# Rotating queries and keys with VectorE's lane shuffle and a GpSimd product instead of TensorE's permutation product

## The chip, the cores and the metric

One core of a Trainium2 chip runs the whole kernel. The time is in device microseconds for one execution. Everything is float32. A large matrix product is made of three products of parts that TensorE takes in one pass each (a high part of weight and input, and a low part of each).

## The reference, cut to what matters

One inference step of a layer with two branches, block-sparse attention with 8 heads of 128 channels and an mLSTM with 4 heads of 256. There are 256 prompt tokens and 8 sample tokens, 264 in all, and the samples attend to a paged cache of 1024 tokens. The change touches one step only, the rotation of normalised queries and keys:

```python
def partial_rope(x, pos):
    half = ROT_DIM // 2                      # ROT_DIM = 32 of 128 channels
    ...
    x1, x2 = xf[..., :half], xf[..., half:ROT_DIM]
    out = jnp.concatenate([x1 * cos - x2 * sin, x2 * cos + x1 * sin, xf[..., ROT_DIM:]], axis=-1)

aq = partial_rope(rms_norm(aq.reshape(B, S, ATT_HEADS, ATT_HD), q_norm_w), pos)
ak = partial_rope(rms_norm(ak.reshape(B, S, ATT_HEADS, ATT_HD), k_norm_w), pos)
```

Only the first 32 of a head's 128 channels are rotated. Channel m of the first 16 is paired with channel m + 16.

## The kernel before, in words

Activations lie with the channels on the 128 partitions and the 264 tokens (`T`) along the free dimension, so a rotation pairs partitions. Each engine has its own list of instructions, and semaphores order them.

**Projections.** 112 blocks of weights (512 KB each, 128 output channels) come in by SyncE's DMA queue, eight ahead. ScalarE splits off the high part (`split_hi`, line 829), VectorE the low part (`split_lo`, line 1082), both three blocks or so ahead of TensorE's 24 products (`project`, lines 545 and 548). ScalarE copies each result out of PSUM and counts `evac`.

**Head stage** (to about 50 us). Blocks 0 to 7 are the eight query heads. For head h ScalarE writes the scaled query to `qT[:, h, :]` and its square to `sq`. One block later, `norm_sums` on TensorE multiplies the square with a matrix of ones (line 553, the sum over the channels) and the query with the permutation `rot` (line 554), and counts `norm_ps`. ScalarE makes the inverse norm `rs` (lines 849 and 850, `rs_ready`). VectorE's `rope_norm` then multiplies the permuted query by the sine (line 1120) and the query by the cosine (1121), adds (1122) and multiplies by the inverse norm (1123), and counts `q_ready`. Between the heads VectorE also works on the gate rows (heads 1 to 3), and at head 3 it counts `rows_ready`. TensorE's product for head g waits for `q_ready` of head g - 2, since it writes the same bank.

After the heads, TensorE projects block 8 and then, in `beside(0)`, waits for `q_ready` of all eight heads and transposes the queries of the sample tokens (line 498).

**GpSimd's list.** After `proj` reaches 2 it issues four key pages and seven value pages of the cache (`keys`, `values`, by line 418), then waits for `rows_ready`, stores the gate rows to DRAM (line 458), waits for that store (`row_put`), loads one row of each kind back to partition 0 (`decay_rows`, lines 442 and 443), waits for these loads and spreads them over the partitions (`spread_rows`, 447 and 448). Then it waits for the sample queries (`qs_ready`), stores them and spreads the first one (465), issues the last value page and enters a loop over the projections, in which it issues the pages for the samples that follow, their queries and the gate rows of the next rounds.

**Four rounds** of 16 projections (lines numbered by i = 0 to 15) follow, each with two attention heads and one mLSTM head: the keys are blocks i = 0 and 1, `keys_side` on TensorE forms their sums and permutation at i = 1 and 3, and VectorE rotates them in `rope_norm` at i = 2 and 4 into `kT[:, n, :]` (`kT_ready`). The tile `hT` holds the sine product in `hT[:, 0, :]`; later in each round it holds mLSTM outputs, until `mlg_ready` is counted. VectorE also scores the cache pages against the sample queries (line 1181) and updates the samples' states (1263). The last 40 projections follow.

Of the kernel before, what the change touches and what calls it, by code (L numbers as in the profile page):

```python
# [33 lines left out]
HEADS = 8  # L34
# [11 lines left out]
ROT = HD // 4  # L46
THETA = 500000.0
# [97 lines left out]
def build(nc, a, o):  # L145
    ctx = ExitStack()
    with ctx:
# [142 lines left out]
        blank, blank_eye = sem("blank"), sem("blank_eye")  # L290
        xsq_act, xsq_dve, xn_ready = sem("xsq_act"), sem("xsq_dve"), sem("xn_ready")
# [108 lines left out]
        def _(pool):  # L400
# [50 lines left out]
            pool.wait_ge(proj, 2)  # L451
            for s in range(KSLOTS):
                keys(s)
            for s in range(VSLOTS - 1):
                values(s)

            pool.wait_ge(rows_ready, 1)
            pool.dma_start(rows_dram, rows[:, :, :].rearrange("p a t -> p (a t)")).then_inc(row_put, 16)
            pool.wait_ge(row_put, 16)
            decay_rows(0)  # L460
# [11 lines left out]
            for g in range(LAST):  # L472
                b = due(g, SELECT)
                if b is not None:
                    pool.wait_ge(mx_ready, b + 1)
                    nc.gpsimd.partition_all_reduce(gmax[:, b, :], mx[:, b % 2, :], P, bass.bass_isa.ReduceOp.max).then_inc(gmax_ready, 1)
                s = key_page(g)
                if s is not None:
                    if s + KSLOTS < NB * PAGES:
                        keys(s + KSLOTS)  # L480
                    if s % PAGES == 0 and 2 <= s // PAGES + 1 < NB:
                        queries(s // PAGES + 1)
                    if s % PAGES == 2 and s // PAGES + 1 < NB:
                        spread_queries(s // PAGES + 1)
                for s in value_loads(g):
                    values(s)
                if g % CHUNKS == 13 and g // CHUNKS + 1 < JOBS:
                    decay_rows(g // CHUNKS + 1)
                if g % CHUNKS == 14 and g // CHUNKS + 1 < JOBS:
                    spread_rows(g // CHUNKS + 1)  # L490
# [3 lines left out]
        def _(pe):  # L494
# [56 lines left out]
            def norm_sums(ss, ro, i, src):  # L551

                mm(ss[:, 0:T], ones, sq[:, i, :], start=True, stop=True)
                mm(ro[:, 0:T], rot, src, start=True, stop=True).then_inc(norm_ps, 1)


            for h in range(HEADS + 1):
# [4 lines left out]
                if h >= 1:  # L562
                    g = h - 1
                    pe.wait_ge(evac, g + 1)
                    if g == 0:
                        pe.wait_ge(boot_r, 16)
                    if g >= 2:
                        pe.wait_ge(q_ready, g - 1)
                    norm_sums(wk[2 * (g % 2)], wk[2 * (g % 2) + 1], g % 2, qT[:, g, :])
# [8 lines left out]
            def keys_side(j, i):  # L578

                if i in (1, 3):  # L580
# [8 lines left out]
                    norm_sums(wk[2 * n], wk[2 * n + 1], n, kT[:, n, :])  # L589
# [486 lines left out]
        def _(dve):  # L1076
# [41 lines left out]
            def rope_norm(x, r, ro, done):  # L1118

                ch.step(V.tensor_tensor(hT[:, 0, :], ro[:, 0:T], sin, ALU.mult))  # L1120
                ch.link(V.tensor_tensor(x, x, cos, ALU.mult))
                ch.link(V.tensor_tensor(x, x, hT[:, 0, :], ALU.add))
                V.tensor_tensor(x, x, r, ALU.mult).then_inc(done, 1)

            for h in range(HEADS):
# [16 lines left out]
                dve.wait_ge(norm_ps, h + 1)  # L1142
                dve.wait_ge(rs_ready, h + 1)
                rope_norm(qT[:, h, :], rs[:, h % 2, :], wk[2 * (h % 2) + 1], q_ready)
# [76 lines left out]
            def keys_side(j, i):  # L1221

                if i in (2, 4):
                    n = i // 2 - 1
                    dve.wait_ge(norm_ps, HEADS + 2 * j + n + 1)
                    dve.wait_ge(rs_ready, HEADS + 2 * j + n + 1)

                    dve.wait_ge(mlg_ready, j)
                    rope_norm(kT[:, n, :], rs[:, n, :], wk[2 * n + 1], kT_ready)
# [222 lines left out]
def constants():  # L1452
# [5 lines left out]
    for m in range(half):  # L1458
        c[m + half, C_ROT + m] = -1.0
# [10 lines left out]
    for s in range(2):  # L1470
        c[s * half:(s + 1) * half, C_COS:C_COS + T] = np.cos(ang)
        c[s * half:(s + 1) * half, C_SIN:C_SIN + T] = np.sin(ang)
# [70 lines left out]
```

## Time and profile before

| | us |
|---|---|
| median of three runs (lowest to highest) | 468.84 (468.48 to 469.5) |
| the profiled execution | 469.01 |
| its span, first to last instruction | 466.9 |
| TensorE busy | 455.6 (98%) |
| VectorE busy | 393.8 (84%) |
| ScalarE busy | 290.5 (62%) |
| GpSimd busy | 100.5 (22%) |
| DMA engines, mean over the span | 323 GB/s |

The granted clock of TensorE is full throughout. In the names of the profile PE is TensorE, PEld its weight loads, DVE is VectorE, ACT is ScalarE, POOL is GpSimd and SP is SyncE; SPq, ACTq and POOLq are their queues of DMA issues and register work. Instructions that an engine merely issues to its DMA queue are not counted as busy. A float32 product takes TensorE two records (x2 in the counts).

### The profile page before, as it was taken

To read this page: it belongs to the slowest core of one execution; us is meant where nothing else is said; L and a number is where in the kernel's file an instruction comes from. 1 tells how busy PE (TensorE), PEld (TensorE's weight loads), DVE (VectorE), ACT (ScalarE), POOL (GpSimd) and SP (SyncE) were. 2 spreads that over 40 slices of the span, in tenths; PEclk is the share of its full clock that TensorE was granted. 3 is DMA by queue.
4 is the path that set the end of the run, shared out by engine and by line. 5 is a ranking of instruction groups with operands and counts; after the bars stand their busy time and mean duration, and the time that the engine had idled before them with its cause. 6 is when DMAs were issued, how large, how long until landed. Compare 5 with 4: busy or idle time off the path is not lost.

```text
span 466.9 us, 11342 instructions
## 1 busy us (share of the span) xinstructions
PE 455.6 (98%) x3855; PEld 414.0 (89%) x3855; DVE 393.8 (84%) x1610; ACT 290.5 (62%) x487; POOL 100.5 (22%) x181
## 2 busy tenths in 40 slices
PE   6999999999999999999999999999999999999997
PEld 4899899897879789888899889889898899899997
DVE  4898899699999799999899999889999946568861
ACT  4866545676984496896485695667958346324430
POOL 2040421013323213422321242312222201000000
PEclk9999999999999999999999999999999999999999
DMA  8899699749999999999999999998999995447511
GB/s 306 324 355 406 173 349 363 237 156 336 320 416 408 388 360 352 412 412 408 409 384 297 405 413 409 411 384 285 403 415 410 409 382 182 162 149 261 181 49 48
DMA packets 44858, 150.91 MB, mean 323 GB/s; under 512 B 6192, under 2 KB 7796, under 8 KB 44672
## 3 DMA queue, kind: packets, MB, share of 16 engines
q1 hardware_dynamic: 20368, 70.77, 41.0%
q0 software_dynamic: 19008, 67.20, 37.4%
q10 hardware_dynamic: 5424, 12.21, 6.9%
q8 instruction: 31, 0.51, 0.4%
q14 instruction: 27, 0.22, 0.1%
HBM read 137.37 MB, written 12.76 MB: 322 GB/s over the span
## 4 chain that ended last, share of the span: by engine, by line
PE 66%; ACT 12%; DVE 9%; DMA 7%; issue 4%; ACTq 1%; SPq 0%; DVEq 0%; POOLq 0%
PE pj L545 25%; PE pj L548 12%; PE wk L545 8%; PE pa L728 4%; PE wk L548 4%; DMA kpages<-in_cache_k 4%; ACT whi L829 3%; DVE kpages L1181 2%; DMA out_C_s<-cslot 2%; ACT L849 2%; DVE wlo L1082 2%; DVE cslot L1263 1%; PE wk L498 1%; PE wk L650 1%; PE wk L684 1%
## 5 line engine op out<-in xcount | busy, mean ns | idle before, releaser
L545 PE MATMUL pj<-xn,whi 128*128 128x264 f32 x1328 | 180.8, 289 | 1.6 <-ACT mqT L987 1.3
L545 PEld LDWEIGHTS pj<-xn,whi 128*128 128x128 f32 x1328 | 168.5, 189 | 10.2 <-issue 6.2
L1082 DVE TENSOR_TENSOR wlo<-wraw,whi 128x1024 fp32r<-128x1024 f32 x112 | 136.2, 1219 | 9.5 <-ACT whi L829 9.1
L829 ACT ACTIVATE whi<-wraw 128x1024 fp32r<-128x1024 f32 x112 | 117.9, 1053 | 21.0 <-PE wk L548 13.5
L1181 DVE CUSTOM_DVE_ANT_0 kpages<-kpages,qbc 128x128 f32<-128x128 f32 x512 | 116.3, 292 | 3.5 <-DMA kpages<-in_cache_k 3.3
L548 PE MATMUL pj<-xn,wlo 128*128 128x264 f32 x664 | 93.9, 284 | 0.7 <-DVE wlo L1082 0.7
L548 PEld LDWEIGHTS pj<-xn,wlo 128*128 128x128 f32 x664 | 85.4, 188 | 1.1 <-DVE wlo L1082 1.1
L418 POOL DMA_DIRECT2D kpages<-in_cache_k x64 | 34.3, 536 | 167.4 <-DVE sco L1181 145.1
L418 POOL DMA_DIRECT2D vpages<-in_cache_v x64 | 33.9, 530 | 60.6 <-issue 38.4
L1181 DVE DVE_READ_ACCUMULATOR2_ANT sco<- 128x1 f32 x512 | 42.1, 82 | 0.0
L728 PE MATMUL pa<-vpages,prob 128*32 128x256 f32 x512 | 33.8, 384 | 1.9 <-ACT prob L887 1.9
L1263 DVE SCALAR_TENSOR_TENSOR cslot<-wk,kc,cslot 128x256 f32<-128x256 f32 x64 | 26.5, 476 | 1.7 <-PE wk L700 1.7
L545 PE MATMUL wk<-xn,whi 128*128 128x264 f32 x192 | 25.9, 287 | 0.0
L728 PEld LDWEIGHTS pa<-vpages,prob 128*32 128x32 f32 x512 | 13.6, 109 | 13.8 <-issue 3.1
L545 PEld LDWEIGHTS wk<-xn,whi 128*128 128x128 f32 x192 | 24.3, 189 | 1.2 <-issue 1.2
L877 ACT ACTIVATE cslot<-cslot,bcg 128x512 f32<-128x512 f32 x32 | 21.2, 711 | 0.0
L922 ACT ACTIVATE att<-att,rsum 128x128 f32<-128x128 f32 x8 | 3.2, 403 | 26.4 <-DVE rsum L1244 26.4
L545 PE MATMUL wk<-mlg,whi 128*128 128x264 f32 x128 | 17.0, 285 | 0.0
L545 PEld LDWEIGHTS wk<-mlg,whi 128*128 128x128 f32 x128 | 16.0, 188 | 0.5 <-issue 0.4
L545 PE MATMUL pj<-mlg,whi 128*128 128x264 f32 x112 | 14.8, 284 | 0.0
L545 PEld LDWEIGHTS pj<-mlg,whi 128*128 128x128 f32 x112 | 14.1, 188 | 0.4 <-issue 0.4
L548 PE MATMUL wk<-xn,wlo 128*128 128x264 f32 x96 | 13.5, 283 | 0.0
(270 smaller groups left out, 609.5 us busy)
## 6 DMA issues: line engine op xcount, KB each, us to landing
wraw<-in_weights SPq DMA_DIRECT2D x112, 512.0 KB, 6.7
kpages<-in_cache_k POOLq DMA_DIRECT2D x64, 512.0 KB, 8.4
vpages<-in_cache_v POOLq DMA_DIRECT2D x64, 512.0 KB, 11.1
cslot<-in_states SPq DMA_DIRECT2D x16, 512.0 KB, 8.8
out_C_s<-cslot ACTq DMA_DIRECT2D x16, 512.0 KB, 8.1
xres<-in_tokens SPq DMA_DIRECT2D x1, 1056.0 KB, 5.6
out_k_p<-kT ACTq DMA_DIRECT2D x4, 256.0 KB, 10.0
out_v_p<-v_nat ACTq DMA_DIRECT2D x4, 256.0 KB, 5.1
```

Source lines behind the costliest of these rows:

```text
L418: return pool.dma_start(tile, src)
L498: return nc.tensor.transpose(out, in_, ident[0:rows_, 0:rows_])
L545: mm(bank[:, 0:T], whi[:, q, k, :], src[:, g, k, :], start=(k == 0 and g == 0), stop=False)
L548: last = mm(bank[:, 0:T], wlo[:, n % WRAW, k, :], src[:, 0, k, :], start=False, stop=(k == KC - 1))
L650: mm(wk[1][g * VC:(g + 1) * VC, 0:MHD], qmask[:, d, b * VC:(b + 1) * VC], cslot[:, b, d, :], start=(half == 0 and d == 0), stop=(half == 1 ...
L728: last = mm(pv[q * VC:(q + 1) * VC, 0:VW], prob[:, b % 2, first:first + VC], vpages[:, s % VSLOTS, q * VW:(q + 1) * VW], start=(pg == 0), ...
L829: A(whi[:, n % WSPLIT], wraw[:, n % WRAW], ACT.Copy).then_inc(whi_ready, 1)
L849: ch.link(A(dst, ss, ACT.Ln, scale=1.0 / width, bias=epsc))
L877: A(cslot[:, b], cslot[:, b], ACT.Copy, scale=bcg[:, 0, j, b:b + 1]).then_inc(fade_ready, 1)
L1082: V.tensor_tensor(wlo[:, n % WRAW], wraw[:, n % WRAW], whi[:, n % WSPLIT], ALU.subtract).then_inc(wlo_ready, 1)
L1181: last = V.tensor_tensor_reduce(k, k, qbc[:, b % 2, h * HD:(h + 1) * HD], 1.0, 0.0, ALU.mult, ALU.add, sco[:, b % 2, pg, h:h + 1])
L1263: last = V.scalar_tensor_tensor(out=cslot[:, b, d, :], in0=row, scalar=kc[:, d, b:b + 1], in1=cslot[:, b, d, :], op0=ALU.mult, op1=ALU.add)
```

## The change

The product with `rot` goes. Instead VectorE shuffles the first 32 partitions with `stream_shuffle`, whose table `SWAP` exchanges the two halves, into `hT[0:32, 0, :]`, and multiplies this by the sine, which carries the sign now. GpSimd multiplies the first 32 partitions by the cosine into `hT[0:32, 1, :]` and counts the new semaphore `scaled`. VectorE waits for `scaled`, adds, waits for `rs_ready`, and multiplies all 128 partitions by the inverse norm. Shuffle and sine product wait for `evac` only.

Since there is one tile for the cosine product, GpSimd waits for the head before to be done (`q_ready`, `kT_ready`) first. GpSimd's other work of the head stage, which stood in one block, is dealt out between the eight products: two pages after each of heads 1 to 5 and one after head 6, the store of the gate rows after head 5's pages, the wait for that store and the two row loads after head 6's page, then head 7's product. TensorE's sum for head g now waits for `rs_ready`.

```diff
+SWAP = [(m + ROT // 2) % ROT for m in range(ROT)]
...
-            pool.wait_ge(proj, 2)
-            for s in range(KSLOTS):
-                keys(s)
-            for s in range(VSLOTS - 1):
-                values(s)
-
-            pool.wait_ge(rows_ready, 1)
-            pool.dma_start(rows_dram, rows[:, :, :].rearrange("p a t -> p (a t)")).then_inc(row_put, 16)
-            pool.wait_ge(row_put, 16)
-            decay_rows(0)
+            pool.wait_ge(blank, 6)
+            pool.wait_ge(boot_r, 16)
+            for h in range(HEADS):
+
+                pool.wait_ge(evac, h + 1)
+                if h:
+                    pool.wait_ge(q_ready, h)
+                pool.tensor_tensor(hT[0:ROT, 1, :], qT[0:ROT, h, :], cos[0:ROT], ALU.mult).then_inc(scaled, 1)
+                if h in (1, 2):
+                    for s in range(KSLOTS // 2):
+                        keys(KSLOTS // 2 * (h - 1) + s)
+                if h in (3, 4, 5, 6):
+                    for s in range(2 * (h - 3), min(2 * (h - 2), VSLOTS - 1)):
+                        values(s)
+                if h == 5:
+                    pool.wait_ge(rows_ready, 1)
+                    pool.dma_start(rows_dram, rows[:, :, :].rearrange("p a t -> p (a t)")).then_inc(row_put, 16)
+                if h == 6:
+                    pool.wait_ge(row_put, 16)
+                    decay_rows(0)
             spread_rows(0)
...
             for g in range(LAST):
+                if g < BODY and g % CHUNKS in (1, 3):
+                    j, n = g // CHUNKS, g % CHUNKS // 2
+                    pool.wait_ge(mlg_ready, j)
+                    pool.wait_ge(kT_ready, 2 * j + n)
+                    pool.wait_ge(evac, HEADS + j * CHUNKS + n + 1)
+                    pool.tensor_tensor(hT[0:ROT, 1, :], kT[0:ROT, n, :], cos[0:ROT], ALU.mult).then_inc(scaled, 1)
...
-                    if g == 0:
-                        pe.wait_ge(boot_r, 16)
                     if g >= 2:
-                        pe.wait_ge(q_ready, g - 1)
-                    norm_sums(wk[2 * (g % 2)], wk[2 * (g % 2) + 1], g % 2, qT[:, g, :])
+                        pe.wait_ge(rs_ready, g - 1)
+                    mm(wk[2 * (g % 2)][:, 0:T], ones, sq[:, g % 2, :], start=True, stop=True).then_inc(norm_ps, 1)
...
-                    norm_sums(wk[2 * n], wk[2 * n + 1], n, kT[:, n, :])
+                    mm(wk[2 * n][:, 0:T], ones, sq[:, n, :], start=True, stop=True).then_inc(norm_ps, 1)
...
-            def rope_norm(x, r, ro, done):
-
-                ch.step(V.tensor_tensor(hT[:, 0, :], ro[:, 0:T], sin, ALU.mult))
-                ch.link(V.tensor_tensor(x, x, cos, ALU.mult))
-                ch.link(V.tensor_tensor(x, x, hT[:, 0, :], ALU.add))
+            def rope(x, r, n, done):
+
+                ch.link(V.stream_shuffle(hT[0:ROT, 0, :], x[0:ROT], SWAP))
+                ch.step(V.tensor_tensor(hT[0:ROT, 0, :], hT[0:ROT, 0, :], sin[0:ROT], ALU.mult))
+                ch.join()
+                dve.wait_ge(scaled, n + 1)
+                ch.link(V.tensor_tensor(x[0:ROT], hT[0:ROT, 0, :], hT[0:ROT, 1, :], ALU.add))
+                dve.wait_ge(rs_ready, n + 1)
                 V.tensor_tensor(x, x, r, ALU.mult).then_inc(done, 1)
...
                 dve.wait_ge(boot_r, 16)
-                dve.wait_ge(norm_ps, h + 1)
-                dve.wait_ge(rs_ready, h + 1)
-                rope_norm(qT[:, h, :], rs[:, h % 2, :], wk[2 * (h % 2) + 1], q_ready)
+                dve.wait_ge(evac, h + 1)
+                rope(qT[:, h, :], rs[:, h % 2, :], h, q_ready)
...
-                    dve.wait_ge(norm_ps, HEADS + 2 * j + n + 1)
-                    dve.wait_ge(rs_ready, HEADS + 2 * j + n + 1)
-
+                    dve.wait_ge(evac, HEADS + j * CHUNKS + n + 1)
                     dve.wait_ge(mlg_ready, j)
-                    rope_norm(kT[:, n, :], rs[:, n, :], wk[2 * n + 1], kT_ready)
+                    rope(kT[:, n, :], rs[:, n, :], HEADS + 2 * j + n, kT_ready)
...
-        c[s * half:(s + 1) * half, C_SIN:C_SIN + T] = np.sin(ang)
+        c[s * half:(s + 1) * half, C_SIN:C_SIN + T] = (2 * s - 1) * np.sin(ang)
```

## Rows read from the trace of the kernel before

**Rows 1.** the page, part 1: busy us of each engine (share), x instructions
```profile
PE 455.6 (98%) x3855; PEld 414.0 (89%) x3855; DVE 393.8 (84%) x1610; ACT 290.5 (62%) x487; POOL 100.5 (22%) x181
```

**Rows 2.** the page, part 4: the chain that ended last, by engine
```profile
PE 66%; ACT 12%; DVE 9%; DMA 7%; issue 4%; ACTq 1%; SPq 0%; DVEq 0%; POOLq 0%
```

**Rows 3.** TensorE's groups by shape: tiles, shapes, count, busy us, mean ns
```profile
L554 PE MATMUL wk<-qT,cst 128*128 128x264 f32 x16 | 4.9, 386 | 0.0
L554 PE MATMUL wk<-kT,cst 128*128 128x264 f32 x16 | 4.9, 386 | 0.0
```

**Rows 4.** the chain by time, 40 to 62 us: start us, us, what
```profile
43.32 0.46 PE wk L554 x2
...
47.89 0.44 DVE qT L1123
...
53.25 0.45 PE wk L554 x2
```

**Rows 5.** timeline, 20 to 50 us: start us, us, engine, line, what
```profile
21.60 0.57 POOL L418 DMA_DIRECT2D kpages<-in_cache_k  x1 [14.34 <-issue]
...
33.51 0.53 POOL L418 DMA_DIRECT2D vpages<-in_cache_v  x1 [0.62 <-issue]
...
34.77 0.52 POOL L458 DMA_DIRECT2D rows_dram<-rows  x1 [0.73 <-DVEq L1140]
...
48.38 0.60 PE L498 MATMUL pa<-cst,qT 128*8 128x128 f32 x4 [0.52 <-DVE qT L1123]
...
49.32 0.51 POOL L442 DMA_DIRECT2D decay<-rows_dram  x1 [14.03 <-DMA rows_dram<-rows]
```

**Rows 6.** DMA issues, 20 to 60 us, median landing; then landings, kpages, vpages
```profile
rows_dram<-rows POOLq DMA_DIRECT2D x1, 8.0 KB, 14.3
...
DMA to landing us min/median/max: 4.4/7.2/8.7
...
DMA to landing us min/median/max: 5.1/11.7/15.2
```

**Rows 7.** timeline of ScalarE and VectorE in the head stage
```profile
21.65 0.42 ACT L850 ACTIVATE rs<-rs 128x264 f32<-128x264 f32 x1
21.98 1.05 ACT L829 ACTIVATE whi<-wraw 128x1024 fp32r<-128x1024 f32 x1
...
23.95 1.23 DVE L1082 TENSOR_TENSOR wlo<-wraw,whi 128x1024 fp32r<-128x1024 f32 x1
...
38.81 0.43 DVE L1123 TENSOR_TENSOR qT<-qT,rs 128x264 f32<-128x264 f32 x1
```

**Rows 8.** timeline at 53 us; then ns min/median/max of two operations
```profile
53.36 1.22 DVE L1082 TENSOR_TENSOR wlo<-wraw,whi 128x1024 fp32r<-128x1024 f32 x1
53.38 2.36 POOL L465 PARTITION_BROADCAST qbc<-qs  x1
...
54.50 1.21 DVE L1166 TENSOR_TENSOR gexp<-wN,cst 8x96 f32<-8x96 f32 x1
...
L434 POOL PARTITION_BROADCAST qbc<-qbc x7: 1294/1300/1468, 69.0 to 315.7; - x7
...
L1193 DVE TENSOR_TENSOR pairs<-gpad x8: 257/258/260, 99.9 to 383.6; 128x96 f32<-128x96 f32 x8
```

**Rows 9.** groups of GpSimd, first microseconds: busy us, mean ns
```profile
L403 POOL MEMSET qmask<- 128x512 f32 x1 | 0.5, 524 | 0.0
L404 POOL MEMSET mvs<- 128x256 f32 x1 | 0.3, 311 | 0.0
```

**Rows 10.** windows: length, busy us (x count), clock, DMA share, GB/s
```profile
28.00:32.00 4.00, 4.00 (x32) 3.84 (x30) 3.83 (x8) 2.81 (x7) 1.59 (x3) 1.00 1.01 408
...
120.00:130.00 10.00, 9.74 (x87) 7.54 (x85) 9.95 (x44) 9.88 (x15) 4.01 (x7) 1.00 0.93 321
```

**Rows 11.** the chain by time, round 1: start us, us, what
```profile
126.66 1.28 ACT L849
...
137.52 0.45 DVE kT L1123
```

More of the change, by code:

```diff
@@ L290, in build @@
         blank, blank_eye = sem("blank"), sem("blank_eye")
+        scaled = sem("scaled")
         xsq_act, xsq_dve, xn_ready = sem("xsq_act"), sem("xsq_dve"), sem("xn_ready")
@@ L549, in project @@
                 last.then_inc(proj, 1)
-            def norm_sums(ss, ro, i, src):
-                mm(ss[:, 0:T], ones, sq[:, i, :], start=True, stop=True)
-                mm(ro[:, 0:T], rot, src, start=True, stop=True).then_inc(norm_ps, 1)
             for h in range(HEADS + 1):
@@ L1458, in constants @@
     for m in range(half):
-        c[m + half, C_ROT + m] = -1.0
+        c[m + half, C_ROT + m] = 1.0
         c[m, C_ROT + m + half] = 1.0
```

## The prediction

> **What bounds the kernel now.** I read the shares of the page first: TensorE is busy 455.6 of 466.9 us, and the chain that ended last runs two thirds over it [rows 1, 2]. So an instruction taken off TensorE is worth its time wherever the chain runs over TensorE, and nothing elsewhere. The groups by shape give the price of what goes: 16 query records and 16 key records of line 554 (two per product), 4.9 us each, 0.31 us a record [rows 3]. In the chain of the stretch 40 to 62 us one product takes 0.45 us, and I use that figure: 16 x 0.45 = 7.2 us is the most that can be gained.
>
> Where does the chain run? Up to the seventh head it is on TensorE, but the last links before 48.38 us are VectorE's: the last head's multiplication by the inverse norm ends at 48.33, and only then does TensorE transpose the sample queries [rows 4]. TensorE had been ready 0.52 us before, at 47.86 [rows 5]. From there through round 0 the chain is TensorE's. At the starts of rounds 1 to 3, where the other six key products lie, it runs over ScalarE (table loads, line 849) and VectorE [rows 11]; between 120 and 130 us VectorE is busy 9.95 of 10 us and ScalarE 9.88 [rows 10].
>
> **What goes from TensorE.** Eight products in the head stage: TensorE would be ready for the sample queries 8 x 0.45 = 3.6 us earlier, at 47.86 - 3.6 = 44.3. In round 0: 2 x 0.45 = 0.9 us on the chain. In rounds 1 to 3: 6 x 0.45 = 2.7 us off the chain; I count 0, the bound is 2.7.
>
> **What VectorE does instead.** Four dependent operations stand where four stood. The removed ones took 0.43 us each by the rows of the last multiplication [rows 7]. The nearest price for the shuffle is the same row, since it streams the same 264 elements a lane; from below, a 96-element operation takes 0.26 [rows 8]. I take 0.45 for the shuffle and about 0.1 more for the whole rotation, since the sine product must now wait for it. The Trainium skill (VectorE: DVE Perf Modes, The perf-mode tier table) gives a shuffle about 2400 ns for 2048 elements; from that an estimate of 0.31 us plus a start for 264. No run here shows a shuffle yet.
>
> **What GpSimd does now, and the port.** It multiplies 32x264 by the cosine, 16 times. Its fills of 256 and 512 columns take 0.311 and 0.524 us, so 0.22 us for 264 columns and 0.10 to start [rows 9]. One pass would be 0.32; two reads and a write in turn are 3 x 0.22 + 0.10 = 0.76; from above stands a spread of 1024 columns, 1.30 [rows 8]. I take 0.75, nearest in kind. The Trainium skill (GPSIMD Engine Reference, Elementwise side-by-side cycle accounting) gives 4497 ns for 2048 elements, an estimate of 0.58 us plus a start, and would have such work stay on VectorE.
>
> GpSimd and VectorE also hold each other up. At 53.38 a spread that takes 1.30 elsewhere took 2.36: it began beside the 1.22 us subtraction of line 1082. The next VectorE operation, 96 elements, took 1.21 instead of 0.26 and ended with the spread [rows 8]. So one waits for the other's whole instruction. The Trainium skill (SBUF — State Buffer, Who interferes with whom) states this as an exclusive lock for two-input VectorE operations; by that rule, the trace agrees. Here each head's end releases both the cosine product and the next subtraction. If VectorE goes first, the product ends 1.25 + 0.75 = 2.0 us later and the sine product waits some 0.3 us for it; if GpSimd goes first, VectorE loses 0.75. I take 0.3, so 0.4 us a head with the 0.1 above.
>
> **The moved DMA issues: the step that decides.** Before, GpSimd issued eleven pages from 21.60 to 33.51 without a break, 1.19 us apart, then the gate rows' store at 34.77. That 8 KB store landed 14.3 us later, behind the pages of its queue (the slowest page took 15.2 from 33.51, so 48.7), and the first of the two loads that wait for it went out at 49.32, its issue taking 0.51 [rows 5, 6]. Nothing of the heads waited for it. After, the same issues stand between the cosine products, and `pool.wait_ge(row_put, 16)` and the two loads stand in the turn of head 6, in front of head 7's product. Head 7's addition, q_ready 8 and TensorE's sample queries are queued behind the landing of that store.
>
> When is it issued? Head 0's inverse norm is there at 22.07 [rows 7], so head 0 is done at about 22.6 instead of 23.9, and GpSimd multiplies head 1 until 23.4. Pages 0 and 1 follow at 24.0 and 25.2. VectorE is the slow one then: with the gate operations of heads 1 to 3 it took from 23.95 to 39.24 for heads 1 to 4 [rows 7], 15.3 us. It may now begin at 23.04, when ScalarE's copy is done [rows 7], and pays 4 x 0.4 more: head 4 is done at 40.0. Head 5's cosine product waits for that and for the subtraction, until 42.0; its two pages go out at 42.6 and 43.8, the store at 44.5.
>
> When does it land? Behind the page of 43.8, and the quickest page took 4.4 us [rows 6]: not before 48.2. By bytes: ten pages, seven weight blocks and one block of states, 9.4 MB, from about 25 us. At the 408 GB/s that a full stretch moves [rows 10] that is 23.1 us, so 48.1. Before, pages landed 2.27 us apart on average; ten from 26.1 would be there at 48.8. I take 48.9, with 47.0 and 51 as ends.
>
> From there: 0.2 to the first load, 1.0 for both issues (2 x 0.51), 0.8 for the product, 0.95 for addition and multiplication: head 7 is done at 51.85, against 48.33. TensorE stands still for 7.5 us from 44.3, and the queries come 3.5 us later than before (1.7 to 5.6 by the ends). Gain and more are gone.
>
> What comes after follows TensorE: the copies of the sample queries shift by 3.5, while the gate rows' spread, 52.0 before, stays where it is and costs nothing more. In round 0 the cosine product of the first key stands behind the spread of the queries, a DMA wait and page 7's issue, about 61.2; VectorE's addition would otherwise be due at 60.6, so it waits 0.6 us. The key scores that need it are four projections away; I count 0, the bound is 0.6.
>
> **The sum.** +3.5 for the heads, -0.9 for round 0, 0 for rounds 1 to 3: +2.6 us. The profiled execution took 469.01 (its span 466.9), 0.17 over the median of 468.84; it becomes 471.6, and the median 471.4.
>
> **The rivals.** *The store is no bound* (lighter queues, or GpSimd ahead of my timetable). Then VectorE's chain sets the end: head 4 at 40.0 and three heads of about 3.3, the last without a subtraction, give 48.3; without the port's price, 46.5. So 0 to -1.8 for the heads, -0.9 for round 0, and up to -1.0 in later rounds: 465.2 to 467.9, likeliest 467.0. For it: before, the store landed at a time when eleven pages had been asked for at once. Against: the quickest page alone already gives 48.2.
>
> *TensorE's time simply goes.* If the store is early, VectorE hides in TensorE's shade and the later rounds give theirs too, the end is 468.84 - 7.2 = 461.6. For it: TensorE at 98%. Against: VectorE paces the heads in 24 to 39 us, and three rounds begin on other engines.
>
> *The port decides in the rounds.* There VectorE works nearly without a gap on two-input operations, and each product takes the port for 0.75 us. Six of them on VectorE's chain, at 0.5 to 0.75, add 3.0 to 4.5 us: 474.4 to 475.9, slower. It decides if VectorE, and not ScalarE, carries the starts of rounds 1 to 3; in round 1 the second key's rotation is on the chain [rows 11], in rounds 2 and 3 it is ScalarE's table loads. That is why it isn't the forecast.
>
> *The gain and the wait cancel*: a store landing at 46.5 to 47.5 together with 1 us from the rounds gives 468 to 469.8, no change.
>
> **How the numbers follow.** A measurement of this kernel can tell about 0.2%, 0.94 us, from no change. Forecast, 469.8 to 473.5: 0.50. Port in the rounds: 0.13. Cancelling: 0.15. Store no bound: 0.16. TensorE's time goes: 0.06. Faster by over 0.2% holds 0.22, within it 0.15, slower 0.63. For 8 in 10 the range leaves out the full gain and the far end of the port: 466.0 to 475.0. The forecast's own range is 469.8 to 473.5.
>
> **What would show it.** In the timeline of the changed kernel: no record of the rotation product, TensorE's period in the head stage 3.4 instead of 3.8 us; the store issued near 44 and landing near 49; the two loads right behind, then head 7's cosine product; TensorE idle for about 7 us before the sample queries, released by VectorE. Cosine products of 0.75 us, longer beside a subtraction. In rounds 1 to 3 no shorter distance between the rounds. The prediction is wrong if the store lands before 46 us, if TensorE's idle time before the queries is under 3 us, or if the rounds after 55 us last shorter by more than 2 us or longer by more than 2 us than before.

## The result and the profile after

The changed kernel took 520.34 us (median, 519.72 to 525.35), the kernel before, on the same chip, 468.82: ratio 1.112 [1.109, 1.116]. The prediction said 471.4 and at most 475.0. The sign was right; the size, 51.5 us, was not foreseen by any of its cases, and twenty times the 2.6 us of its sum.

The page of the changed kernel: busy time by engine, the slices of TensorE and of its granted clock, and the chain that ended last.

```profile
PE 462.2 (89%) x3823; PEld 416.9 (80%) x3823; DVE 397.6 (77%) x1626; ACT 290.4 (56%) x487; POOL 122.7 (24%) x197
...
PE   7994576999978999986999984679999999999997
...
PEclk9998697999997999998999997779999999999999
...
PE 54%; DVE 21%; issue 10%; ACT 8%; POOL 2%; DMA 2%; POOLq 2%; ACTq 0%; DVEq 0%
```

Against [rows 1, 2]: the span grew by 51.2 us to 518.1, and yet no engine has much more to do. TensorE is busy 6.6 us more, with 32 records fewer; VectorE 3.8 more, GpSimd 22.2 more. The new time is waiting, and it comes in holes of TensorE's row: a deep one at slices 4 and 5 (39 to 65 us), others near 80, 160, 230 and 310 to 340 us, with a lower clock in each. The share "issue" of the chain, time in which an engine waited for nothing that the profile shows, went from 4% to 10%.

The waits of the changed kernel name the engine (us in total, times, longest):

```profile
POOL hT L490 <- issue: 41.7, 5, 9.3
DVE kT L1134 <- POOL hT L490: 36.7, 5, 11.2
...
PE pj L566 <- DVE wlo L1092: 32.1, 8, 8.4
```

Read it from the top. Ahead of five of the eight cosine products of keys (line 490) GpSimd stood for 8.3 us on average, and nothing that the profile shows released it. VectorE's addition (1134) waited for those five products, and behind it on VectorE stood the split of the next weights (1092), for which TensorE's second pass (566) waited. The timeline of the first one:

```profile
67.95 0.58 POOL L420 DMA_DIRECT2D vpages<-in_cache_v  x1 [0.68 <-issue]
76.88 0.73 POOL L490 TENSOR_TENSOR hT<-kT,cst 32x264 f32<-32x264 f32 x1 [8.35 <-issue]
...
77.72 0.42 DVE L1134 TENSOR_TENSOR kT<-hT 32x264 f32<-32x264 f32 x1 [9.85 <-POOL hT L490]
...
81.62 2.13 PE L566 MATMUL pj<-xn,wlo 128*128 128x264 f32 x8 [6.66 <-DVE wlo L1092]
...
97.61 1.31 POOL L436 PARTITION_BROADCAST qbc<-qbc  x1 [7.78 <-issue]
```

What GpSimd did in the 8.35 us is seen only when one line's instructions are listed with its queue's: `MODIFY_POOL_CONFIG`, two records of 37 ns, the last at 68.6 us, then nothing until 76.88. The rows of the changed kernel (count, ns min/median/max, first to last start):

```profile
L490 POOLq MODIFY_POOL_CONFIG  x10: 37/37/42, 68.6 to 328.0; - x10
L436 POOLq MODIFY_POOL_CONFIG  x4: 37/37/37, 90.1 to 318.6; - x4
L494 POOLq MODIFY_POOL_CONFIG  x6: 37/37/37, 164.5 to 353.6; - x6
L449 POOLq MODIFY_POOL_CONFIG  x2: 22/22/22, 56.5 to 56.6; - x2
```

They come in pairs, so eleven times; a twelfth pair, ahead of the first product, lies at 7.6 us under the wait for the inputs. In the kernel before there is one pair, at the first spread, which went out 1.6 us later, when its DMA had landed:

```profile
L447 POOLq MODIFY_POOL_CONFIG  x2: 37/37/37, 50.4 to 50.4; - x2
```

The pattern: a pair stands ahead of a product when the last operation was a spread or a maximum over the partitions (lines 436, 449, 494), and ahead of one of those when the last was a product. Page issues between them don't matter. Where only fills had run, as in the kernel before, the pair is cheap. I read it as GpSimd exchanging the code of one kind of operation for that of the other, and call a pair with its hole a loading. The load itself is not seen: the two DMA queues marked "instruction" moved 0.49 and 0.23 MB here, 0.51 and 0.22 before. The Trainium skill (GPSIMD Engine Reference, 2.1 Instruction dispatch) describes such a load: the first call of freshly loaded code pays about 6 us, with no instruction to show for it. Here the holes are 5.8 to 9.3 us long, and ten of the eleven are over 7.0 us, more than that figure.

The head stage of the changed kernel, where the prediction had its one large term:

```profile
43.48 0.56 POOL L469 DMA_DIRECT2D rows_dram<-rows  x1
...
54.58 0.52 POOL L444 DMA_DIRECT2D decay<-rows_dram  x1 [8.57 <-DMA rows_dram<-rows]
...
55.59 0.75 POOL L460 TENSOR_TENSOR hT<-qT,cst 32x264 f32<-32x264 f32 x1
...
57.40 1.02 PE L516 MATMUL pa<-cst,qT 128*8 128x128 f32 x4 [12.39 <-DVE qT L1136]
...
59.55 2.85 PE L563 MATMUL pj<-xn,whi 128*128 128x264 f32 x16
...
62.19 0.55 POOL L449 PARTITION_BROADCAST decay<-decay  x1 [5.84 <-issue]
```

The chain is the predicted one: store, its landing, loads, head 7's product, sample queries. But TensorE stood for 12.4 us, not 7.5, and what it did next took longer than in [rows 5]: 1.02 us where line 498 took 0.60. The windows (length, busy us of PE, PEld, DVE, ACT, POOL, granted clock, DMA share, GB/s) show TensorE at its lower level of 1.2 GHz in and after the hole, and partly after the hole of round 0:

```profile
50.00:60.00 10.00, 2.60 (x14) 1.63 (x15) 3.47 (x8) 0.00 (x0) 1.75 (x3) 0.50 0.27 106
...
80.00:90.00 10.00, 8.38 (x52) 7.66 (x53) 9.86 (x49) 1.34 (x2) 2.63 (x4) 0.76 0.67 212
```

To place the 51.2 us I take ScalarE's copy of a round's first keys as the round's start, and the last `mrs` (line 850 before, 860 after) as the end of round 3.

| | before | after | difference | pairs in it |
|---|---|---|---|---|
| start to round 0 | 47.98 | 45.12 | -2.9 | |
| round 0, with the end of the heads | 68.87 | 89.82 | +20.9 | 3 |
| round 1 | 74.50 | 81.08 | +6.6 | 2 |
| round 2 | 73.31 | 79.95 | +6.6 | 2 |
| round 3 | 74.04 | 94.42 | +20.4 | 4 |
| last projections | 128.2 | 127.7 | -0.5 | |

The first row is TensorE's gain, 2.9 us for eight products (3.6 predicted). The second row holds three pairs and the wait for the row store; e5, below, separates the two. Rounds 1 to 3 are longer where pairs are, though not evenly: 3.3 us for each pair in rounds 1 and 2, 5.1 in round 3.

### The profile page after: what moved, and what is told of

It is laid out like the page before. It is cut to its first block, busy times and chain, and to the rows that moved or that the text cites. A ratio compares the mean times of both kernels' runs of the same rounds, so it can differ in the third digit from the quotient of the medians.

```text
span 518.1 us, 11376 instructions
## 1 busy us (share of the span) xinstructions
PE 462.2 (89%) x3823; PEld 416.9 (80%) x3823; DVE 397.6 (77%) x1626; ACT 290.4 (56%) x487; POOL 122.7 (24%) x197
## 4 chain that ended last, share of the span: by engine, by line
PE 54%; DVE 21%; issue 10%; ACT 8%; POOL 2%; DMA 2%; POOLq 2%; ACTq 0%; DVEq 0%
PE pj L563 18%; PE pj L566 9%; PE wk L563 8%; DVE kpages L1193 7%; DVE wlo L1092 5%; PE wk L566 4%; PE pa L738 4%; DMA rows_dram<-rows 2%; ACT whi L839 2%; PE wk L516 1%; ACT L859 1%; POOLq L417 1%; DVE cslot L1273 1%; PE wk L660 1%; PE wk L694 1%
## 5 line engine op out<-in xcount | busy, mean ns | idle before, releaser
L566 PE MATMUL pj<-xn,wlo 128*128 128x264 f32 x664 | 99.1, 294 | 32.1 <-DVE wlo L1092 32.1
L1193 DVE CUSTOM_DVE_ANT_0 kpages<-kpages,qbc 128x128 f32<-128x128 f32 x512 | 117.6, 294 | 0.1
L566 PEld LDWEIGHTS pj<-xn,wlo 128*128 128x128 f32 x664 | 89.5, 196 | 33.8 <-DVE wlo L1092 33.8
L420 POOL DMA_DIRECT2D kpages<-in_cache_k x64 | 36.7, 573 | 129.4 <-DVE sco L1193 118.9
L420 POOL DMA_DIRECT2D vpages<-in_cache_v x64 | 34.4, 538 | 46.5 <-issue 28.0
L738 PE MATMUL pa<-vpages,prob 128*32 128x256 f32 x512 | 35.6, 400 | 0.8 <-ACT prob L897 0.7
L1134 DVE TENSOR_TENSOR kT<-hT 32x264 f32<-32x264 f32 x8 | 3.4, 421 | 36.8 <-POOL hT L490 36.7
L937 ACT ACTIVATE att<-att,nm 128x128 f32<-128x128 f32 x8 | 3.2, 395 | 31.4 <-DVE nm L1249 31.4
L997 ACT ACTIVATE mkT<-pj 128x264 f32<-128x264 f32 x8 | 3.1, 384 | 27.5 <-PE pj L566 27.5
L460 POOL TENSOR_TENSOR hT<-qT,cst 32x264 f32<-32x264 f32 x8 | 13.4, 1674 | 18.4 <-ACT sq L855 10.9
```

The costliest lines, as they stand in the source:

```text
L420: return pool.dma_start(tile, src)
L460: pool.tensor_tensor(hT[0:ROT, 1, :], qT[0:ROT, h, :], cos[0:ROT], ALU.mult).then_inc(scaled, 1)
L566: last = mm(bank[:, 0:T], wlo[:, n % WRAW, k, :], src[:, 0, k, :], start=False, stop=(k == KC - 1))
L738: last = mm(pv[q * VC:(q + 1) * VC, 0:VW], prob[:, b % 2, first:first + VC], vpages[:, s % VSLOTS, q * VW:(q + 1) * VW], start=(pg == 0), ...
L1193: last = V.tensor_tensor_reduce(k, k, qbc[:, b % 2, h * HD:(h + 1) * HD], 1.0, 0.0, ALU.mult, ALU.add, sco[:, b % 2, pg, h:h + 1])
```

## The experiments

Times are medians, ratios stand to the kernel before on the same chip. e1 to e4 ran on one chip, e5 to e11 on another; the kernel before took 468.9 us on the first and 468.7 and 468.8 on the second, so a difference between two experiments can be off by 0.2 us for that alone. "All on VectorE" means that the cosine product stands on VectorE too, ahead of the shuffle; nothing else of the rotation differs from the changed kernel.

**e1, what makes GpSimd load.** The kernel before, with one 8x8 operation that nobody waits for at i = 1 and 3 of each round, of another kind in each round.

```diff
...
+                    if j == 0:
+                        pool.memset(spare[:, 0, :], 0.0).then_inc(spared, 1)
+                    if j == 1:
+                        pool.tensor_copy(spare[:, 0, :], ident[0:8, 0:8]).then_inc(spared, 1)
+                    if j == 2:
+                        pool.tensor_scalar(spare[:, 0, :], ident[0:8, 0:8], 2.0, None, ALU.mult).then_inc(spared, 1)
+                    if j == 3:
+                        pool.tensor_tensor(spare[:, 0, :], ident[0:8, 0:8], ident[0:8, 0:8], ALU.mult).then_inc(spared, 1)
...
```

> The kernel before, with eight GpSimd operations on 8x8 elements added that nobody waits for: at projections 1 and 3 of each round, a fill in round 0, a copy in round 1, a multiplication by a number in round 2, a product of two tensors in round 3. Theory S (loading code): GpSimd stands still for about 8 us whenever an elementwise product follows a spread or a reduction over the partitions, and again for 6 to 8 us before the next spread, however small the operation; so at least round 3 shows an idle time of 7 to 9 us before its first product and one more before the next spread or reduction, and pages are issued late behind it: 470 to 490 us. Rival P (port and size): the product was late because VectorE holds the port; 64 elements then cost under 1 us each and the time stays at 469. The fill, the copy and the multiplication tell which kinds need the loading; S does not say.

Measured: 483.48, a single execution. The timeline of GpSimd in e1:

```profile
56.65 0.10 POOL L479 MEMSET spare<- 8x8 f32 x1
...
126.18 0.43 POOL L481 COPY spare<-cst 8x8 f32<-8x8 f32 x1
...
209.58 0.27 POOL L483 TENSOR_SCALAR spare<-cst 8x8 f32<-8x8 f32 x1 [9.90 <-issue]
...
230.94 0.39 POOL L489 PARTITION_ALL_REDUCE gmax<-mx  x1 [8.56 <-issue]
...
305.33 1.11 POOL L485 TENSOR_TENSOR spare<-cst 8x8 f32<-8x8 f32 x1 [8.04 <-issue]
```

The records ahead of the two operations with two inputs:

```profile
L485 POOLq MODIFY_POOL_CONFIG  x4: 37/37/37, 278.6 to 297.4; - x4
```

Fill and copy load nothing; an operation with a scalar and one with two inputs do, and the spread or maximum after them loads back. 64 elements wait 8 to 10 us as 8448 do, so the wait has nothing to do with size. Six loadings were added (one ahead of the scalar form, two ahead of the two-input form, three back) and the kernel is 14.6 us slower, though no other engine waits for the results: 2.4 us each on average. I put that down to GpSimd's list, which issues pages and spreads queries late; this one execution doesn't show it apart.

**e2, all on VectorE.** GpSimd's list as before.

```diff
...
-                    pool.tensor_tensor(hT[0:ROT, 1, :], kT[0:ROT, n, :], cos[0:ROT], ALU.mult).then_inc(scaled, 1)
...
+                    ch.step(V.tensor_tensor(hT[0:ROT, 1, :], x[0:ROT], cos[0:ROT], ALU.mult))
...
```

> The changed kernel with the cosine product on VectorE and GpSimd's list as before the change: the rotation product is gone from TensorE, and GpSimd has no product. Theory S: no GpSimd idle time over 5 us without a DMA or another engine behind it, and the 51 us are gone. What is left is TensorE's gain of up to 7.2 us against 16 more VectorE operations of 0.45 us, 7.2 us: 465 to 470 us, likeliest 467. Rival W (the waits come from the shuffle or from the new order of the waits on VectorE and TensorE): still over 480.

Measured: 470.27 (469.12 to 470.58), ratio 1.0027 [1.0009, 1.0045], 0.3 us above the expected range. One pair of records is left, as before. So the shuffle and VectorE's other operations are not what costs; 50 of the 51.5 us are GpSimd's product and what was moved for it. TensorE waited 4.0 us ahead of the queries, since VectorE now paces it, and then ran slowly:

```profile
49.40 1.02 PE L500 MATMUL pa<-cst,qT 128*8 128x128 f32 x4 [4.04 <-DVE qT L1124]
```

**e3, GpSimd's product for the heads only,** in the changed kernel's order; the keys on VectorE.

> The changed kernel with the cosine product of the round keys on VectorE; the head stage stays on GpSimd. Theory S: the head stage costs what it costs in the changed kernel, head 7 done at 57.3 instead of 48.3 us (9.0), 1.7 us of half clock, and one loading before the spread of the gate rows; nothing in the rounds: 477 to 482 us. My forecast's mechanism (the row store's wait) says the same of the head stage. Rival P (port) gives 470 to 473.

Measured: 478.34 (477.60 to 479.56), 1.0206 [1.0186, 1.0227]. The wait for head 7 is 11.9 us against 4.0 in e2, and the kernel 8.1 us slower than e2: the two agree. Two pairs are left, one in the first 8 us and the one at the first spread, now behind a product.

**e4, the wait for the row store put behind head 7's product,** otherwise the changed kernel.

```diff
-                if h == 6:
+                if h == 7:
                     pool.wait_ge(row_put, 16)
                     decay_rows(0)
```

> The changed kernel with the wait for the row store and the two row loads moved behind head 7's cosine product. If the store's wait in front of head 7 makes TensorE's 12.4 us of idle time, it falls to under 5 us (VectorE's chain ends head 7 at about 48.5) and the time falls by 7 to 12 us to 508 to 513, since the rounds keep their loadings. If the idle time comes from something else (the port, the DMA queues), it stays at 520. If the whole loss came from the head stage, it falls under 475.

Measured: 525.9 (520.51 to 527.8), 1.12 [1.114, 1.126]; a miss. The times overlap with those of the changed kernel (519.72 to 525.35), so the 5.6 us between the medians are not clear of noise; the gain of 7 to 12 us that was expected is excluded. The wait ahead of the queries fell from 12.4 to 3.8 us, as expected, and nothing of it reached the end. The next rows of e4 show what came in its place:

```profile
62.34 0.55 POOL L449 PARTITION_BROADCAST decay<-decay  x1 [6.86 <-issue]
...
63.35 0.42 DVE L1283 TENSOR_TENSOR decay<-decay,cst 128x256 f32<-128x256 f32 x1 [7.06 <-POOL floor L450]
```

The spread of the gate rows follows the product with a loading between them, and VectorE, which reached its multiplication (1283) sooner, waited for it 7.06 us instead of 2.38. After that the rounds go by GpSimd's list, which had not become earlier: five key products still wait, 9.2 us on average (46.0 us in all, 41.7 in the changed kernel), and TensorE's wait for line 1092 grew from 32.1 to 43.0 us. I read this as a gain ahead of a list that is the bound being lost in it.

**e5, a copy for the product.** The changed kernel with GpSimd copying where it multiplied; the cosine is left out of the rotation.

```diff
...
-                    pool.tensor_tensor(hT[0:ROT, 1, :], kT[0:ROT, n, :], cos[0:ROT], ALU.mult).then_inc(scaled, 1)
+                    pool.tensor_copy(hT[0:ROT, 1, :], kT[0:ROT, n, :]).then_inc(scaled, 1)
...
```

> The changed kernel with a plain copy on GpSimd in place of each cosine product: same tile, same waits, same place in the queue; the cosine is left out of the rotation. In the first call a copy of 64 elements needed no loading of code and a product of 64 elements needed 8 us. Theory S (loading code): the 42 us of the rounds go, the head stage keeps its wait for the row store: 477 to 482 us. Rival Q (the cosine operation stands behind page issues and DMA waits in GpSimd's queue and VectorE waits for that, whatever the operation): still 510 to 520 us. Rival P (port): the copy has one input, so it would be faster only by its own length, under 1 us each: 505 to 515.

Measured: 475.68 (475.46 to 476.35), 1.0145 [1.0123, 1.0168], 1.3 us under the expected range. Order, waits, sizes and the exchange through `hT` are those of the changed kernel; only the kind of the operation differs, and with it its length, and 44.7 of the 51.5 us are gone. A copy of a key took 0.42 us where the product took 0.74, so the shorter operation can make up 16 x 0.3, about 5 us of the 44.7, at the most. The copies still meet the subtractions: seven of the heads' eight took 1.0 to 2.5 us. One pair of records is left, 0.8 us ahead of the first spread:

```profile
L449 POOLq MODIFY_POOL_CONFIG  x2: 29/29/29, 55.1 to 55.1; - x2
```

The end of its head stage in the timeline:

```profile
53.64 0.51 POOL L444 DMA_DIRECT2D decay<-rows_dram  x1 [8.87 <-DMA rows_dram<-rows]
...
56.09 1.02 PE L516 MATMUL pa<-cst,qT 128*8 128x128 f32 x4 [10.68 <-DVE qT L1136]
```

What remains, 6.9 us, is the head stage's wait for the store: 10.7 us of it, as the chain in the prediction has it. By the measure of the table above, round 0 with the end of the heads takes 80.75 us in e5, 11.9 more than before and without a loading that anything waits for; rounds 1 to 3 take 73.30, 73.31 and 74.05, no more than before. So of the 20.9 us in the table's second row 11.9 are the store's wait, and its three pairs leave about 9.

**e6, the row store early.** e3, with the store issued after head 4's product, ahead of its pages, and the wait and loads behind head 7's.

```diff
+                if h == 4:
+                    pool.wait_ge(rows_ready, 1)
+                    pool.dma_start(rows_dram, ...).then_inc(row_put, 16)
...
-                if h == 6:
+                if h == 7:
                     pool.wait_ge(row_put, 16)
                     decay_rows(0)
```

> Heads on GpSimd, keys of the rounds on VectorE (478.3 us in the first call), with the store of the gate rows issued after head 4's product, ahead of head 4's pages, and its wait and the row loads behind head 7's product. If the head stage's 9 us are the store's landing behind the pages, it lands by 46 us, TensorE's wait before the sample queries falls from 11.9 to about 4 us, one loading of 5.8 us before the spread remains and holds VectorE up to about 56 us: 471 to 474 us. If the loading hides behind other work: 469 to 470. If the port makes the heads slow, it stays at 478.

Measured: 470.11 (469.35 to 471.12), 1.0022 [1.0008, 1.0036]: 8.2 us better than e3, all that GpSimd's heads had cost. Two things differ from e3, the place of the store and that of its wait, and no run separates them here; in e4 the wait's place alone took TensorE's wait from 12.4 to 3.8 us, as it is in e6.

```profile
39.50 0.61 POOL L466 DMA_DIRECT2D rows_dram<-rows  x1
...
47.74 0.56 POOL L444 DMA_DIRECT2D decay<-rows_dram  x1
...
56.53 0.55 POOL L449 PARTITION_BROADCAST decay<-decay  x1 [7.73 <-DMA floor<-rows_dram]
```

Issued 4.5 us earlier than in e3, the store had landed (at 45.7) when the loads' turn came at 47.74. The pair of records ahead of the spread is still there, at 49.1, but the second row load landed only at 55.8, 7.5 us after its issue, and the spread went out 0.7 us later: the loading lay under that wait, and the 5.15 us that VectorE waited for the spread can't be put down to it. So the heads' cosine products, 1.1 to 1.7 us each for those beside VectorE's work, cost nothing against e2, and head by head the port is no cost that reaches the end.

**e7, keys on VectorE, heads on TensorE** as before.

> The kernel before with the rotation product kept on TensorE in the head stage, and the round keys rotated on VectorE alone (shuffle, sine, cosine, add: one operation more than before). From the chain before: TensorE gains 0.9 us in round 0 and 2.7 us off the chain in rounds 1 to 3; VectorE pays 8 x 0.45 = 3.6 us, of which 0.9 in round 0. Likeliest 468.5, between 467.5 and 470.5. If the head stage is what made the all-VectorE kernel 1.4 us slower, this one is at or below the kernel before; if VectorE's extra operations in the rounds did, it is at 470.

Measured: 469.28 (467.4 to 470.58), 1.0008 [0.9992, 1.0025]: the same as before. Taking the key products from TensorE in all rounds neither gains nor costs anything that these runs can tell.

**e8, e2 with TensorE kept busy.** An unread product per head stands where the rotation's stood, with the old wait for `q_ready`.

```diff
...
+                    mm(wk[2 * (g % 2) + 1][:, 0:T], rot, sq[:, g % 2, :], start=True, stop=True).then_inc(norm_ps, 1)
...
```

> The all-VectorE kernel (470.3 us) with a product of the same size kept on TensorE in each head, whose result nobody reads. There TensorE waited 4.0 us for the last head and then ran at half clock: the first projection after it took 3.83 instead of 2.3 us and the transposes 2.5 instead of 1.3. Theory C (the clock makes it slower than before): TensorE's wait shrinks to about 1.5 us, the granted clock stays full, and the time falls by 1.5 to 2 us to 468.3 to 468.8, though TensorE has 3.6 us more work. Rival: without a clock effect more work on TensorE can only leave it at 470.3 or above.

Measured: 468.31 (467.23 to 472.52), 0.9998 [0.9978, 1.0018]. TensorE had more to do than in e2, and the kernel was 2.0 us faster by the medians; by the ratios it is 1.4 us, and the two intervals just overlap, so the gain is likely and its size open. Its row of the queries, in e8:

```profile
48.92 0.60 PE L500 MATMUL pa<-cst,qT 128*8 128x128 f32 x4 [0.96 <-DVE qT L1129]
```

The queries start at about the same time as in e2 (48.92 and 49.40), after a wait of 0.96 instead of 4.04 us, and take 0.60 instead of 1.02 us: the granted clock was 1.00 from 48 to 56 us, where e2 has 0.50 from 50 to 54. At round 0's first sum of squares of a key, e2 is 3.0 us behind (56.17 and 53.18): 0.5 of the start, 0.9 in the transposes and 1.6 in the projection. The old wait for `q_ready` spreads TensorE's work too, so the product alone is not what was tested. Here a TensorE freed for a few microseconds ahead of a wait gained nothing and lost its clock.

**e9, the keys only on GpSimd;** heads on VectorE, GpSimd's list of the head stage as before.

> Query heads rotated wholly on VectorE, GpSimd's list of the head stage as before; the keys of the rounds as in the changed kernel, with GpSimd's cosine product. Loading theory (each change between an elementwise product and a spread or reduction on GpSimd costs it about 8 us, and the rounds' list becomes the bound): the ten changes of the rounds are all still there, the head stage's 8 us (478.34 - 470.27) are gone, so 520.3 - 8.1 = 512 us, range 505 to 516, with single waits of about 8 us marked as issue ahead of five of the eight key products and ahead of the spreads and reductions that follow. Rival: heads and rounds act on each other, the late head stage being what pushes the rounds' list behind: then well under 500 us. Rival of the port (the products hold VectorE up, nothing is loaded): under 480 us.

Measured: 516.79 (514.49 to 518.52), 1.100 [1.097, 1.103], just over the expected range. Ten loadings are there in the rounds, and the time is 46.5 us over e2. The head stage adds only 3.6 to it in the changed kernel, where alone it cost 8.1: my reading is that with the list as the bound part of its lateness is not seen. Against the port rival, which wanted under 480, the result is plain.

**e10, GpSimd's product in round 2 only,** everything else on VectorE.

```diff
-if g < BODY and g % CHUNKS in (1, 3):
+if g // CHUNKS == 2 and g % CHUNKS in (1, 3):
```

> All rotation on VectorE except the two keys of round 2, whose cosine product is GpSimd's. Loading theory: only round 2 has changes of kind, one or two to the product and as many back, so two to four records of waiting of about 8 us each on GpSimd and none elsewhere; what of it is seen at the end is at most 6.6 us in the middle rounds of the changed kernel (its rounds 1 and 2 are 6.6 us longer each), so 470.3 + 4 to + 8: 474 to 478 us. Rival: what costs is not the change of kind but a slower GpSimd everywhere: 470.3 + a quarter of 43 = 481 us or more. Rival of the port alone: 470.3 to 472.

Measured: 478.88 (476.9 to 480.8), 1.0201 [1.0166, 1.0237]: 8.6 us over e2, 0.9 over the expected range. GpSimd's timeline of e10:

```profile
208.77 0.74 POOL L480 TENSOR_TENSOR hT<-kT,cst 32x264 f32<-32x264 f32 x1 [8.01 <-issue]
...
213.51 0.76 POOL L480 TENSOR_TENSOR hT<-kT,cst 32x264 f32<-32x264 f32 x1
...
236.27 0.40 POOL L484 PARTITION_ALL_REDUCE gmax<-mx  x1 [8.61 <-issue]
```

Its records at these two lines:

```profile
L480 POOLq MODIFY_POOL_CONFIG  x2: 33/35/37, 200.8 to 200.8; - x2
...
L484 POOLq MODIFY_POOL_CONFIG  x2: 37/37/37, 227.9 to 227.9; - x2
```

The second product, with no spread before it, waits for nothing. One change of kind and one back cost 8.6 us at the end. Against e2, and by the measure of the table above, round 2 is 6.1 us longer (79.38 and 73.30) and round 3, which has no pair, 4.6 (79.29 and 74.68), while rounds 0 and 1 are not: a slower GpSimd everywhere is ruled out, and part of the price shows a round later. The mean price per loading agrees in three comparisons: 8.6 / 2 = 4.3 (e10 against e2), 46.5 / 10 = 4.7 (e9 against e2), 42.0 / 10 = 4.2 (the changed kernel with twelve pairs against e3 with two). It is a mean and no constant: e1 has 2.4, and the rounds of the changed kernel 3.3 to 5.1. About half of what GpSimd loses in the ten holes of the changed kernel's rounds (80.2 us) is seen at the end.

**e11, the kernel before with only round 0's two keys on VectorE.**

> The kernel before with only the two keys of round 0 rotated wholly on VectorE; heads and rounds 1 to 3 on TensorE as before. The prediction's step for round 0 (two products of 0.45 us leave a chain that runs over TensorE): 468.8 - 0.9 = 467.9 us. Rival (VectorE's added operations take it back, as in the kernel with all keys on VectorE, 469.28): 468.8 us or a little more.

Measured: 467.69 (466.91 to 469.65), 0.9977 [0.9962, 0.9991]: 1.15 us faster than before, and the only version of these that beats it clear of noise. It is small: the interval reaches from 0.1 to 0.4%.

## Why the prediction was wrong

**TensorE's products: right in kind.** They were put at 0.45 us each, worth something only where the chain runs over TensorE. Eight in the head stage brought round 0's start 2.9 us forward (3.6 predicted); two in round 0 bring 1.15 us in e11 (0.9); in rounds 1 to 3 they bring nothing (e7 is 1.6 us slower than e11).

**VectorE's part: right.** The shuffle took 0.43 to 0.45 us (0.45 taken). The Trainium skill (VectorE: DVE Perf Modes, The perf-mode tier table) led to an estimate of 0.31 us and a start; the measured time allows that. With the whole rotation on VectorE the kernel is 1.4 us slower than before (e2) and with the keys' alone 0.5 (e7, within noise), TensorE's savings taken off.

**GpSimd's product and the port: the durations were right, and they don't matter.** Its two groups in the changed kernel (ns min/median/max):

```profile
L490 POOL TENSOR_TENSOR hT<-kT,cst x8: 731/742/1692, 76.9 to 335.7; 32x264 f32<-32x264 f32 x8
...
L460 POOL TENSOR_TENSOR hT<-qT,cst x8: 752/1718/2791, 18.4 to 55.6; 32x264 f32<-32x264 f32 x8
```

Alone it takes 0.74 us (0.75 predicted), beside a subtraction 1.72 in the median (the prediction had 2.0 from release to end). The rival of the port in the rounds (+3.0 to 4.5) didn't show: seven of the eight key products took 0.73 to 0.76 us and one 1.69, and with copies in their place rounds 1 to 3 were as long as before (e5). In the heads e6 and e2 differ by 0.2 us. What the port costs in the rounds is not measured by itself; eight products of 0.74 us are 5.9 us in all.

**The step that failed: "cosine products of 0.75 us" as the whole price of a product on GpSimd.** The prediction read what GpSimd multiplies and what it spreads as durations only, and never asked whether it can go from one kind to the other. The trace of before had no elementwise product among its spreads, so no row showed the change of kind; it did have one pair of `MODIFY_POOL_CONFIG`, which I had not listed, and the section of the Trainium skill that is named above was not weighed. What stood in its place: eleven loadings of 6 to 9 us, ten of them in the rounds. VectorE's additions waited 36.7 us for five of the products, where the prediction put 0 and a bound of 0.6. With the products' extra length over a copy, at most 5 us, the loadings make 44.7 us (e5); by the ten of the rounds alone it is 42.0 (e3).

**The gate rows' spread "stays where it is and costs nothing more": wrong.** Head 7's product now stands between the loads and the spread, so a hole of 5.8 us follows it where the pair of before stood 1.6 us ahead of the spread, under a DMA's wait: 62.19 instead of 52.0. In e6, where it lies under the landing of the row loads, it costs nothing; in e3 and the changed kernel its share was not taken apart.

**The store as the bound of the heads: right in kind, 5.4 us short in size.** Issued at 43.48 (44.5 predicted), landed at 54.3 (48.9, end 51); TensorE waited 12.4 us (7.5), and head 7 was done at 57.3 (51.85). The term that was mis-sized is the work ahead of the store at full rate. The DMA rate of the changed kernel in 20 to 60 us, one number for each us:

```profile
GB/s 41 131 385 8 74 274 262 229 377 348 365 246 311 348 377 283 303 389 365 373 397 397 365 381 422 418 414 418 406 410 412 412 188 29 20 1 1 0 0 0
```

The trace's packets show the store itself: its four packets of 2,048 bytes ran from 51.0 to 51.4 us, when about ten pages' bytes had gone over its queue, so it did come behind the pages as the prediction says. Up to 51.4 us the engines had moved 9.5 MB from 25 us on, the 9.4 that were counted, but at 358 GB/s and not at the 408 of [rows 10], which only the stretch after 40 us reaches (404): 26.4 us instead of 23.1. The landing was then counted 2.9 us after the last packet, a term for which the sum had 0.8 us at most (48.1 to 48.9).

**The fall of the clock was not in the sum.** After a 4 us wait it put e2 2.5 us behind e8 in round 0, of which the medians leave about 1.5 at the end. Of the 51.5 us it may be more, since the clock falls in several stretches; no run isolates it there.

So of the 51.5 us 44.7 go with the kind of GpSimd's operation, nearly all of them loadings (e5), and the other 6.9 are mostly the store's landing (10.7 us of wait less what TensorE had gained). The sign was no luck, since the predicted wait alone makes the kernel slower; but even without the loadings e5's 475.7 lies just outside the stated range, for the store's term alone. None of the prediction's cases held the loadings. One sum among its rivals is off by its own terms: 40.0 and three heads of 3.3, the last without its 1.25 us subtraction, give 48.7 and not 48.3, which touches neither forecast nor range. Its line "wrong if the rounds after 55 us last longer by more than 2 us" is the one that caught it: the sample queries came 9.0 us later, and the other 42 us of the 51.2 lie behind them.

## What to carry to other kernels

Before giving an engine a new kind of operation, list the kinds that it already runs and look for `MODIFY_POOL_CONFIG` records between them: on GpSimd an elementwise product among spreads and reductions over partitions cost about 8 us of its time at each change of kind, whatever its size, and 4 to 5 us at the end on average in this kernel (2.4 where no other engine waited for it, none where a DMA's wait lay over it), while fills, copies and DMA issues cost none. If such work must go there, keep it in one stretch without the other kind, or choose a kind that needs no loading. An instruction that a store's landing holds up, in front of work on the critical path, is worth moving behind it, but only if the list behind it is not the next bound (e6, which also issues the store earlier, gained 8 us, e4 nothing).

## What the runs showed of the hardware that I had not expected

- Changing GpSimd from spread or maximum to a two-input or scalar operation and back: 5.8 to 10.3 us of idle time, nearly always marked as issue (10.3 in e9), behind a pair of `MODIFY_POOL_CONFIG` records; for 8x8 as for 32x264. Fill and copy none: with only these run before it, the first spread went out 0.8 to 2.5 us behind its pair (e5 and e1), each time under the wait for its DMA.
- The load starts when the operation before it on GpSimd is done, not earlier: the records lie at 68.6 us, behind the page issue of 67.95, and the product 8.3 us later. In e6 they lie at 49.1, before the row loads had landed (55.8), and the spread followed at 56.5, so it can run under a wait of its own instruction.
- TensorE's clock was at the 1.2 GHz level after idle stretches of 4.0 us (e2) and 12.4 us (changed kernel), and not after one of 0.96 us (e8). After 3.8 us in e6 the first transposes still took 0.60 us and the next 0.95, with a granted clock of 0.50 from 50 to 52 us; after 3.8 us in e4 the first took 1.01 already.
